# Score, exponential and turn order at the start of three attention stages, and one rotary step in two, in a four-layer transformer kernel

## What is computed

```python
def first_block(x, ...):                      # layers "A", twice
    h = rms_norm(x, norm_mix_w[i])
    q, k, v, z, xbc_raw, dt_raw = split(h @ w_in[i])
    q, k = axial_rope(rms_norm(q)), axial_rope(rms_norm(k))
    attn_out = blocked_gqa(q, k, v)           # 8 query heads, 2 key heads, full softmax over 512 keys
    ssd_out = ssd_mixer(z, xbc_raw, dt_raw, ...)   # 5-tap conv, silu, two-way chunked scan, gate by silu(z), norm
    x = x + concatenate([attn_out, ssd_out]) @ w_out[i]
    x = x + (silu(h2 @ w_gate[i]) * (h2 @ w_up[i])) @ w_down[i]     # h2 = rms_norm(x)

def second_block(x, ...):                     # layers "B", twice
    qa, ka, va, qb, kb, vb = split(rmsnorm(x) @ w_in[l])
    ya = windowed_gqa_sink(rope(qa), rope(ka), va, sink[l])         # banded: |i - j| <= 128
    yb = diff_attention(rope(qb), rope(kb), vb, lam)                # softmax 1 minus lam times softmax 2
    x = x + concatenate([ya, rmsnorm(yb)]) @ w_out[l]
    x = x + (silu(conv3(gate)) * val) @ w_down[l]
```

## Time and profile before

| | us |
|---|---|
| median of the runs | 2444.28 |
| lowest and highest of three | 2441.65, 2444.98 |
| the profiled execution | 2441.04 |
| its span | 2439.3 |

### The profile page before, as it was taken

How to read it: one execution, slowest core, us unless ns; L and a number is a source line. 1 busy time by engine, 2 the same in 40 slices (tenths; PEclk the granted TensorE clock), 3 DMA queues, 4 the chain that set the end, 5 groups by cost and what they waited for, 6 DMA issues and landing times.

```text
span 2439.3 us, 30895 instructions
## 1 busy us (share of the span) xinstructions
PE 2389.9 (98%) x12492; PEld 1970.8 (81%) x12492; DVE 1427.6 (59%) x1950; ACT 934.6 (38%) x1468; POOL 274.7 (11%) x199
## 2 busy tenths in 40 slices
PE   8999999999999999999999999999999999999999
PEld 7777888888877788888887778888888777888887
DVE  6876444445587644343567766555466776645554
ACT  5574322223446532222444752222234475322222
POOL 2013100001200300000232410000012212000000
PEclk9999999999999999999999999999999999999999
DMA  5110222223211122222221112222232111222222
GB/s 188 69 36 28 94 104 88 102 90 118 88 70 36 35 89 101 104 89 101 104 88 69 36 35 94 96 104 93 97 108 99 53 36 53 87 104 87 104 91 99
DMA packets 31101, 205.32 MB, mean 84 GB/s; under 512 B 3440, under 2 KB 3568, under 8 KB 7408
## 3 DMA queue, kind: packets, MB, share of 16 engines
q1 hardware_dynamic: 30960, 203.35, 23.4%
HBM read 201.24 MB, written 2.10 MB: 83 GB/s over the span
## 4 chain that ended last, share of the span: by engine, by line
PE 89%; DVE 7%; ACT 1%; issue 1%; DVEq 1%; ACTq 0%; POOL 0%; DMA 0%; SPq 0%
PE bank L1656 26%; PE bank L1658 26%; PE bank L1657 26%; PE bank L1778 2%; PE bank L1839 2%; PE bank L1815 2%; DVE a_conv L1077 1%; DVE neg_max L1450 1%; PE bank L1761 1%; DVE b_p L1462 1%; PE bank L1826 1%; PE bank L2061 0%; PE bank L2259 0%; PE bank L2078 0%; PE bank L2235 0%
## 5 line engine op out<-in xcount | busy, mean ns | idle before, releaser
L818 DVE TENSOR_TENSOR w_lo<-w_raw,w_hi 128x2048 fp32r<-128x2048 f32 (+1 forms) x180 | 411.2, 2284 | 392.3 <-ACT w_hi L341 391.8
L1656 PE MATMUL bank<-h_ffn_hi,w_hi 128*128 128x512 f32 x1408 | 548.6, 390 | 0.0
L1658 PE MATMUL bank<-h_ffn_hi,w_lo 128*128 128x512 f32 x1408 | 547.8, 389 | 0.0
L1657 PE MATMUL bank<-h_ffn_lo,w_hi 128*128 128x512 f32 x1408 | 547.7, 389 | 0.0
L341 ACT ACTIVATE w_hi<-w_raw 128x2048 fp32r<-128x2048 f32 (+1 forms) x180 | 340.9, 1894 | 462.6 <-PE bank L1658 433.8
L1658 PEld LDWEIGHTS bank<-h_ffn_hi,w_lo 128*128 128x128 f32 x1408 | 264.3, 188 | 55.3
L1657 PEld LDWEIGHTS bank<-h_ffn_lo,w_hi 128*128 128x128 f32 x1408 | 264.3, 188 | 54.7
L1656 PEld LDWEIGHTS bank<-h_ffn_hi,w_hi 128*128 128x128 f32 x1408 | 264.3, 188 | 54.4
L1656 PE MATMUL bank<-act_hi,w_hi 128*128 128x512 f32 x704 | 273.9, 389 | 0.0
L1657 PE MATMUL bank<-act_lo,w_hi 128*128 128x512 f32 x704 | 273.9, 389 | 0.0
L1658 PE MATMUL bank<-act_hi,w_lo 128*128 128x512 f32 x704 | 273.9, 389 | 0.0
(11 more groups left out here) (325 smaller groups left out, 3413.5 us busy)
## 6 DMA issues: line engine op xcount, KB each, us to landing
w_raw<-weights SPq DMA_DIRECT2D x184, 1024.0 KB, 4.8
w_raw<-weights SPq DMA_DIRECT2D x4, 544.0 KB, 3.8
w_raw<-weights SPq DMA_DIRECT2D x8, 256.0 KB, 6.2
residual<-x_in SPq DMA_DIRECT2D x8, 256.0 KB, 6.2
x_out<-residual SPq DMA_DIRECT2D x8, 256.0 KB, 2.0
cst<-consts SPq DMA_DIRECT2D x1, 966.0 KB, 9.3
par_b<-params_b SPq DMA_DIRECT2D x1, 627.0 KB, 10.2
par_a<-params_a SPq DMA_DIRECT2D x1, 244.0 KB, 2.6
```

Of the source, the lines that this page charges most:

```text
L818: nc.vector.tensor_tensor(w_lo[s][:, cols], w_raw[s][:, cols], w_hi[s][:, cols].bitcast(F32), ALU.subtract).then_inc(w_ready, 1)
L1656: mm(out, ahi, bhi, start=start, stop=False)
L1657: mm(out, ahi, blo, start=False, stop=False)
L1658: return mm(out, alo, bhi, start=False, stop=stop)
```

## The change

1. **A, rotary step.** `rope` is cut into `rope_products` and `rope_finish`. The products of tile 3 run between `conv_start(6)` and `conv_taps(5)`, the rest after `conv_start(7)`.
2. **A, attention.** Scores of step 1 are computed with those of step 0 inside z's last tile. ACT has the exponentials of steps 0 and 1 ahead of the turned queries. Step 0's probabilities are turned in step 1 and step 1's in step 2. The third and fourth query tiles are turned through banks 4 and 3.
3. **A, mixer.** `exponents(2)` goes to bank 0 and is issued before the states; from there the loop issues `exponents` one ahead: w issues 2w+3 and 2w+4 where it issued 2w+2 and 2w+3. Banks 5 and 6 still alternate. ACT's list is unchanged.
4. **A, tail.** Three of the four `out_rows` of the second half move behind the last `y_products`.
5. **B, banded attention.** ACT does the exponentials of step 0 before the second half of the value eviction. Step 0's probabilities are turned in step 1. Both copies of step 0 stand ahead of step 1 on ACT and DVE.
6. **B, differential attention.** Scores 0 are issued behind step 17 of the banded loop; DVE's `diff_max(0)` goes ahead of `normalise(3)`, and ACT's two `diff_exp(0, c)` go ahead of `out_hi(3)`. `diff_scores` holds what stood inline, with the same matmuls.

```diff
-                    nc.scalar.activation(A[f"a_e{w % 2}{d}"][:, :], bank[E_BANKS[u % 2]][:, :], ACT.Exp).then_inc(dec_ready, 1)
+                    nc.scalar.activation(A[f"a_e{w % 2}{d}"][:, :], bank[exponent_bank(u)][:, :], ACT.Exp).then_inc(dec_ready, 1)
...
                 probs, pts = pair_tiles(A, "a_p"), pair_tiles(A, "a_pt")
-                for i in range(20):
-                    if i == 1:
-                        for m in (4, 5):
-                            turned_hi(m)
+                pair_exp(lay, 0, 0, 512, probs)
+                pair_exp(lay, 0, 1, 512, probs)
+                pair_exp(lay, 1, 0, 512, probs)
+                pair_exp(lay, 1, 1, 512, probs)
+                turned_hi(4)
+                pair_copy(lay, 0, 512, pts)
+                turned_hi(5)
+                for i in range(2, 20):
                     if 4 <= i < 12:
                         split_quarter(lay, g0 + 9 + i // 4, i % 4)
                     if i < 16:
                         pair_exp(lay, i, 0, 512, probs)
-                    if 2 <= i < 18:
+                    if 3 <= i < 18:
                         pair_copy(lay, i - 2, 512, pts)
                     if i < 16:
                         pair_exp(lay, i, 1, 512, probs)
...
-                for half in range(2):
-                    evict_pair(g0 + 7, half, lambda t: B["b_vb"][:, t, :])
+                evict_pair(g0 + 7, 0, lambda t: B["b_vb"][:, t, :])
...
+                    pair_exp(lay, 0, par_, window(0)[1] * P + 1, probs)
+                evict_pair(g0 + 7, 1, lambda t: B["b_vb"][:, t, :])
+                pair_copy(lay, 0, window(0)[1] * P, pts)
+                for i in range(1, 20):
...
-                    if 2 <= i < 18:
+                    if 3 <= i < 18:
                         pair_copy(lay, i - 2, window((i - 2) // 4)[1] * P, pts)
...
+                    if i == 18:
+                        diff_exp(0, 0)
+                        diff_exp(0, 1)
                     if i >= 7 and i % 4 == 3:
                         out_hi(lay, (i - 7) // 4, B["b_on"], B["b_ot_hi"])
...
-                    if i < 16:
+                    if 1 <= i < 16:
                         diff_exp(i, 0)
...
+                rope_finish(count, t, H, col, sqs, m1, rope_products(t, sqs, m1, pieces, table, axes))
+
+            def rope_products(t, sqs, m1, pieces, table, axes):
...
+                return parts
+
+            def rope_finish(count, t, H, col, sqs, m1, parts):
...
                 conv_taps(3)
                 split_lo(g0 + 8)
                 conv_start(5)
-                rope_a(3)
                 conv_taps(4)
                 conv_start(6)
+                last_tile = products_a(3)
                 conv_taps(5)
                 conv_start(7)
+                finish_a(3, last_tile)
                 split_lo(g0 + 9)
                 conv_taps(6)
...
                 pts = pair_tiles(A, "a_pt")
                 pair_max(lay, 0)
+                pair_max(lay, 1)
                 take_gate()
-                for m in (4, 5):
-                    turned_lo(m)
-                for i in range(1, 19):
+                turned_lo(4)
+                pair_copy(lay, 0, 512, pts)
+                turned_lo(5)
+                for i in range(2, 19):
...
-                    if 2 <= i < 18:
+                    if 3 <= i < 18:
...
                 window_max(0)
+                pair_copy(lay, 0, window(0)[1] * P, pts)
                 for i in range(1, 19):
...
-                    if 2 <= i < 18:
+                    if 3 <= i < 18:
                         pair_copy(lay, i - 2, window((i - 2) // 4)[1] * P, pts)
+                    if i == 18:
+                        diff_max(0)
                     if i >= 6 and i % 4 == 2:
                         normalise(lay, (i - 6) // 4, B["b_r"], B["b_on"])
                     if i >= 8 and i % 4 == 0:
                         out_lo(lay, (i - 8) // 4, B["b_on"], B["b_ot_hi"], B["b_ot_lo"])
...
-                    if i < 16:
+                    if 1 <= i < 16:
                         diff_max(i)
                     if i == 0:
                         out_lo(lay, 3, B["b_on"], B["b_ot_hi"], B["b_ot_lo"])
...
-                    if 1 <= i < 16:
+                    if (1 if windows else 2) <= i < 16:
                         pair_scores(lay, i, windows, q_of, k_of, masked)
-                    if 2 <= i < 18:
-                        u = i - 2
+                    if i in turn_step:
+                        u = turn_step.index(i)
...
                     pe.wait_ge(t_free, base + 4)
                     pair_scores(lay, 0, False, query_rows, key_rows, False)
+                    open_bank(0, g0 + 10)
+                    open_bank(1, g0 + 10)
+                    pair_scores(lay, 1, False, query_rows, key_rows, False)
...
                 turn_query(2)
-                turn_query(3)
-
-                def second_scores():
-                    open_bank(0, g0 + 10)
-                    open_bank(1, g0 + 10)
+
+                def first_turns():
+                    open_bank(2, g0 + 10)
+
+                def turn_last_query():
+                    open_bank(3, g0 + 10)
+                    turn_query(3)
 
                 def third_scores():
                     pe.wait_ge(t_free, base + 5)
-                    open_bank(2, g0 + 10)
-                    open_bank(3, g0 + 10)
...
-                    j = E_BANKS[u % 2]
-                    if u >= 2:
-                        pe.wait_ge(dec_ready, 16 * lay + u - 1)
+                    j = exponent_bank(u)
+                    if u >= 3:
+                        pe.wait_ge(dec_ready, 16 * lay + (u - 2 if u < 5 else u - 1))
...
-                               {1: second_scores, 2: third_scores, 3: fourth_scores, 17: last_but_one, 18: last}, {})
+                               {1: first_turns, 2: third_scores, 3: fourth_scores, 17: last_but_one, 18: last}, {1: turn_last_query},
+                               [1, 2] + list(range(4, 18)))
+                exponents(2)
...
                     if w < 7:
-                        exponents(2 * w + 2)
                         exponents(2 * w + 3)
+                    if w < 6:
+                        exponents(2 * w + 4)
...
                         out_rows(0, w - 2)
-                    if w >= 6:
+                    if w == 6:
                         pe.wait_ge(sm_ready, 4 * lay + 4)
-                        out_rows(1, 2 * w - 12)
-                        out_rows(1, 2 * w - 11)
+                        out_rows(1, 0)
                     y_products(w)
+                for k in range(1, 4):
...
                         open_bank(j, g0 + IN_B)
+                    open_bank(2, g0 + IN_B)
 
                 def third_scores():
                     pe.wait_ge(qk_raw, 10 + 10 * l + 4)
-                    open_bank(2, g0 + IN_B)
...
-                                7: turn_first_key, 10: turn_second_key, 11: lambda: turn_diff(6), 14: turn_last_key})
+                                7: turn_first_key, 10: turn_second_key, 11: lambda: turn_diff(6), 14: turn_last_key, 17: lambda: diff_scores(0)},
+                               [1] + list(range(3, 18)))
...
+                    if 1 <= i < 16:
+                        diff_scores(i)
...
+def exponent_bank(u):
+
+    return 0 if u == 2 else E_BANKS[u % 2 if u < 2 else (u - 3) % 2]
...
-TURN_A = (5, 6, 7, 4, 7, 4, 5, 6, 5, 6)
+TURN_A = (5, 6, 7, 4, 4, 3, 5, 6, 5, 6)
```

More of the change, by code:

```diff
@@ L1793, in pair_scores, with pair_attention @@
                         last.then_inc(s_done, 1)
-            def pair_attention(lay, windows, q_of, k_of, v_of, masked, probs, pts, between, behind):
+            def pair_attention(lay, windows, q_of, k_of, v_of, masked, probs, pts, between, behind, turn_step):
                 base = 32 * lay
@@ L2214, in turned, with diff_scores @@
                     pe.wait_ge(t_free, base + 6 + n)
+                def diff_scores(i):
+                    t, h = divmod(i, 4)
+                    if i >= 2:
+                        pe.wait_ge(de_done, 32 * l + 2 * (i - 2) + 2)
+                    ts_ = slice(t * P, (t + 1) * P)
+                    for n, (qt, kt) in enumerate(((h_mix_hi, kt_hi), (h_mix_hi, kt_lo), (h_mix_lo, kt_hi))):
+                        for c in range(2):
+                            rows = slice(c * HD, (c + 1) * HD)
+                            last = mm(bank[DS_BANKS[i % 2][c]][:, :], qt[rows, 4 + h, ts_], kt[rows, h, :],
+                                      start=(n == 0), stop=(n == 2))
+                            if n == 2:
+                                last.then_inc(ds_done, 1)
                 pair_attention(lay, True, query_rows, key_rows,
@@ L2226, in _ @@
                 for i in range(19):
-                    if i < 16:
-                        t, h = divmod(i, 4)
-                        if i >= 2:
-                            pe.wait_ge(de_done, 32 * l + 2 * (i - 2) + 2)
-                        ts_ = slice(t * P, (t + 1) * P)
```

(9 more changed lines are left out.)

47 lines of the change are left out of this document (27 added, 20 removed).

## The result

The changed kernel takes 2454.28 us (median of 5 runs, 2451.65 to 2456.02), the kernel before 2441.65 in 5 runs and 2441.4 over all 29 that ran beside the first experiments. The ratio is 1.0049, with an interval of 1.0037 to 1.0062: slower by 0.5%, some 12 us. Forecast were 2451, 2442 to 2461. The profiled execution of the changed kernel took 2454.62 us with a span of 2452.8, 13.5 more than the span before. Code lines have moved: `exponents` is now L2062 and L2063, `y_products` L2114, the turning of queries and outputs L1794, scores L1811, the turning of probabilities L1848, differential scores L2265 and turning L2290, `out_lo` L982, `diff_max` L1464, `diff_coef` L1495, ACT's `diff_exp` L764.

What follows compares the result with a forecast made beforehand. PE was taken as the bound, busy nearly all the time. Two A layers at +1.0, two B layers at +2.0 and +4 for the clock made +10 on 2441.04: 2451 us, 8-in-10 range 2442 to 2461.

Steps and rivals of the forecast that it cites:

- The two queue losses: A mixer (part 3), +4.6 us a layer from waits behind ACT's list; B differential start (part 6), +1.7 from late `out_lo(3)`.
- the term for `split_lo`: A rotary step: PE would reach `split_lo(g0 + 9)` sooner than DVE has it; wait 0 to 0.5, taken as 0.1 us.
- both waits: A mixer: PE waits 3.8 us before `exponents(8)` for decay 6, and 1.7 before `exponents(14)` for decay 12.
- The gain of 1.2 at the states: A mixer: earlier `exponents(2)` removes the 0.8 us wait for scan states and about 0.4 of two others.
- the 1.8 us wait of `turn_diff` in one piece: B banded start: step 2 has no turning to fill the gap, so the second `turn_diff` waits about 1.8 us.
- the walk: B differential start, queue by queue: DVE idle 1.4 us before `out_lo(3)`, `diff_max(1)` 3.9 after `diff_max(0)`, 1.7 later than before.
- two further drops: Whole kernel: two more falls of the granted clock at 2.0 us each, +4; bounds none and five at 3.
- the four long waits: PE waits of 3.8 us in each A layer and some 4.4 of 5.3 us idle at each B layer's differential start.
- The case of a drop at every long wait: Rival for the whole kernel: every long wait drops the clock, 2441 + 6 + 5 x 3.0 = 2462 us; chance 0.10.
- the B layers' queues: B banded start +0.3 us and differential start +1.7, so +2.0 in each of two layers, without clock drops.
- the ramps: A rotary step and attention start (parts 1 and 2): gains of 1.4 and 1.0 us in each layer.

Runs made afterwards that it cites:

- the first experiments: silu_early, silu_ynorm, undo_mixer and undo_diff, the first four follow-up kernels; the kernel before took 2441.39 us in 29 runs beside them.
- silu_early: Changed kernel with ACT's `late_silu` moved from behind decay(5) to between decay(4) and `take_scores(1)`: 2443.85 us, ratio 1.0014.
- silu_ynorm: silu_early with ACT's `y_norm(0)` also moved behind decay(12): 2443.68 us, ratio 1.0012.
- undo_mixer: Changed kernel with the issue order and banks of `exponents` as in the kernel before, moved `out_rows` kept: 2443.03 us, ratio 1.0007.
- tail_kept: ramps_alone plus part 4, output rows 1 to 3 of the second half behind the last two products: 2437.71 us, ratio 0.9984.
- squares_first: tail_kept with ACT's squares of the fourth chunk ahead of the scaling of the third: 2434.50 us, ratio 0.9973.
- undo_banded: Changed kernel with part 5, the banded start, alone undone: 2450.63 us, ratio 1.0038.
- best_out_lo_moved: Changed kernel with silu_ynorm's two edits, undo_banded's and out_lo_moved's, part 6 kept: 2440.49 us, ratio 0.9993.
- undo_diff: Changed kernel with part 6, the start of the differential attention, as before the change: 2449.37 us, ratio 1.0031.
- out_lo_moved: Changed kernel with DVE's `out_lo(3)` moved behind `diff_max(1)`: 2451.03 us, ratio 1.0038.
- best_of_parts: Changed kernel with silu_ynorm's two edits, undo_banded's and undo_diff's: 2437.75 us, ratio 0.9985.
- ramps_alone: Kernel before with parts 1 and 2 alone: 2436.33 us, ratio 0.9980.
- rotary_alone: Kernel before with part 1 alone, the last tile's rotary step in two: 2437.64 us, ratio 0.9988.

## Why the prediction was right, and where it was not

The sum came out near: +10 forecast, +13.5 of span measured, within the range. The two queue losses, which were the reason to expect a slower kernel, are both there with the causes described. Step by step:

**Parts 1 and 2** were forecast at 2.4 us a layer and measured at 2.15 and 2.60. In part 1 the term for `split_lo` was mis-sized: 0.1 forecast, 0.84 in the first A layer and 0.4 in the second. The gain there is 0.85 and 1.44, not 1.4 twice; part 2 gave 1.3 and 1.2 for 1.0.

**Part 3** has both waits, 3.66 and 1.59 for 3.8 and 1.7, and their causes are shown by silu_early and silu_ynorm. They cost less than they are long: the second cost 1.1. (silu_early's 4.9 and 4.6 for the first hold the drop as well.) The gain of 1.2 at the states was wrong. It shows as a vanished wait and not as time: undo_mixer has the wait of 0.8 back and the same 46.42.

**Part 4**, 1.2 forecast, is worth nothing by itself (tail_kept). I had written that `y_products(7)` would come up against `mixer(7)` and still counted a gain. The step that failed is reading the 1.72 us before the last turning as PE's to fill: PE was waiting for a chain that runs from DVE's `a_y` through ACT, DVE and POOL. Matmuls moved under that wait don't shorten it; the 0.4 us by which `a_y` did come sooner was lost in ACT's order (squares_first).

Parts 3 and 4 together were put at +3.4 in a layer. The mixer grew by 6.0 and 5.7 with its drop. undo_banded has half the drop (3.4 us) and 1.1 less in the first layer and 0.6 less in the second, so without any it would be some 3.8 and 4.4 by my estimate (6.0 - 2 x 1.1 and 5.7 - 2 x 0.6, from the table). The estimate takes the two halves of a drop to cost the same, which no run shows; a drop of 3.4 us cost 1.6 in best_out_lo_moved. That 3.8 and 4.4 are near the forecast 3.4 is partly luck: two errors offset each other, waits counted at their full length and gains that weren't there.

**Part 5**, forecast +0.3 in both layers: +0.8 and +0.5 at full clock, and the 1.8 us wait of `turn_diff` in one piece came as described. The size was too small in the first layer, where I had compared with a stage that ran with a drop.

**Part 6**, forecast +1.7: +2.0 and +1.7, with every row of the walk there (3.87 after `diff_max(0)` for 3.9, 1.44 of idleness for 1.4). undo_diff gives the two stages back whole (45.58 and 45.30), and out_lo_moved confirms the cause for three quarters of the loss in the first layer and three fifths in the second.

**The clock**, forecast as two further drops at 2.0. There were five for one, and the one before is gone. A drop of 6.8 us cost 1.5 to 2.1 (50.62 against 49.11 in undo_diff, 18.87 against 17.02, 51.22 against 49.11), near the forecast 2.0; one of 3.4 cost 0.3 to 1.6 (49.46 against 49.11 in best_of_parts, 48.01 against 46.43 in best_out_lo_moved, where PE was busy 3.20 of 3.20 us in it). So the mixers paid 2.2 and 1.3 by the estimate above, the differential starts 2.1 and 0.9, the second banded start 1.0, and the first got 1.9 back: 5.6 net for the forecast 4. The error was the count: two further drops, where each of the four long waits had one and the second banded start a fifth; that one went away at the first banded start was luck for the sum. The case of a drop at every long wait was itself added up with five drops, where four waits had been counted; with four it stands at 2459.

**All together.** By the stages, the mixers grew by 11.7 us, the banded starts by 0.4, the attentions by 3.7 and the differential starts by 3.0, and the mixers began 5.2 sooner (2.5 and 2.6, by the first decay matmul): 13.5, which is the whole difference of the spans. Against the forecast of 10 the clock makes 1.6 of the difference, parts 3 and 4 make 1.4, the B layers' queues 1.0 (2.8 + 2.2 for 4.0), and the ramps take 0.4 off.

The Trainium skill, "TensorE: Matmul & The Clock Gate", section "HAM oscillation", lets gaps of PE re-throttle it. The trace agrees for the mixers, where the clock fell within the wait of 3.66. The shorter waits went either way: a drop came with both waits of 2.6 at the differential starts, and with one of the two waits of 1.8 in the banded starts. The rule doesn't tell why the wait of 2.2 before the differential scores goes without a drop in the kernel before and with one in ramps_alone, with the same instructions around it (49.49 and 51.47 in the table).

Not settled is why a drop lasts 3.4 us in one kernel and 6.8 in the next at the same place. No experiment took the clock's state apart from the order of the work, and no kernel was traced in more than one execution.

## What to carry to other kernels

When a matmul engine issues work one step earlier, walk the list of the engine that frees its bank: one item that stood one place too early there (a function with two table loads) made a loss of some 10 us over two layers with the clock drops behind it, and moving that item alone took it back. A wait in front of an engine is only worth filling if its own work ends it; follow the chain behind the wait to its slowest link, and shorten that. Moved matmuls gave nothing here until one swap on ScalarE let the chain use the 0.4 us that they had won. Where short waits stand at the edge of a clock drop, price each part with and without it, compare stages only at the same clock, and look at the clock of all runs before a median is believed to 2 us.

## What was not expected of the hardware

- Low-clock stretches had two lengths in these traces, 3.4 and 6.8 us, and the length of the wait didn't decide which: 6.8 with a wait of 3.66 in the mixer of the changed kernel, 3.4 with one of 3.65 in undo_banded.
- The same instructions with the same waits ran at either clock. The first banded start had its drop in the kernel before, tail_kept and best_of_parts (18.9 us), and none in rotary_alone, ramps_alone and undo_banded (17.0). What these had edited lies in other stages, so the work there differed only in when it ran, and the stage still differed by 1.9 us, more than most parts of this change are worth. Whether the edits moved the drop or it falls differently in every execution isn't shown; the runs of the kernel before, all of the same code, spread over 6.7 us with their clock.
